# A two-block mixer, GLA and expert kernel: work of the chunked scan moved between engines, other stages reordered

## The reference

```python
def step(state, xs):                       # hgrn2_scan, per chunk
    qc, kc, vc, lfc = xs
    cum = jnp.cumsum(lfc, axis=-2)
    o_inter = einsum('bhtd,bhde->bhte', qc * exp(cum), state)
    diff = cum[:, :, :, None, :] - cum[:, :, None, :, :]
    decay = exp(where(tril[:, :, None], diff, -inf))
    scores = einsum('bhtd,bhsd,bhtsd->bhts', qc, kc, decay)
    o_intra = einsum('bhts,bhse->bhte', scores, vc)
    k_dec = kc * exp(cum_last - cum)
    state = exp(cum_last)[..., None] * state + einsum('bhsd,bhse->bhde', k_dec, vc)
```

## Time and profile before

| | us |
|---|---|
| runs before: median (lowest, highest) | 1871.67 (1871.23, 1877.39) |
| profiled execution, its own time | 1871.47 |
| its span | 1869.7 |
| PE busy | 1817.9 |
| PEld busy | 1346.8 |
| POOL busy | 978.1 |
| VectorE busy | 782.6 |
| ScalarE busy | 549.4 |

### The profile page before, as it was taken

How to read it: one execution, slowest core, us unless ns; L and a number is a source line. 1 busy time by engine, 2 the same in 40 slices (tenths; PEclk the granted TensorE clock), 3 DMA queues, 4 the chain that set the end, 5 groups by cost and what they waited for, 6 DMA issues and landing times.

```text
span 1869.7 us, 22394 instructions
## 1 busy us (share of the span) xinstructions
PE 1817.9 (97%) x9105; PEld 1346.8 (72%) x9105; DVE 782.6 (42%) x1154; ACT 549.4 (29%) x1037; POOL 978.1 (52%) x547
## 2 busy tenths in 40 slices
PE   7998999999999999999999999999999999999998
PEld 6887888788888888888777888878744444433456
DVE  4375777734524301422676565433221222221234
ACT  5534557522422101211233444332230000000025
POOL 6499958467378878897565896437500000000022
PEclk9999999999999999999999999999999999999999
DMA  6231125223123222333322322114999999999991
GB/s 210 86 90 46 46 79 181 68 68 109 39 91 92 100 101 91 102 113 92 114 79 69 90 90 83 53 57 148 387 385 410 428 427 427 428 428 427 421 373 56
DMA packets 82918, 335.83 MB, mean 180 GB/s; under 512 B 6528, under 2 KB 8320, under 8 KB 67712
## 3 DMA queue, kind: packets, MB, share of 16 engines
q1 hardware_dynamic: 79296, 322.47, 46.1%
q10 hardware_dynamic: 3520, 11.93, 1.7%
HBM read 328.08 MB, written 6.29 MB: 179 GB/s over the span
## 4 chain that ended last, share of the span: by engine, by line
PE 80%; POOL 7%; DMA 5%; DVE 4%; ACT 2%; issue 1%; SPq 0%; ACTq 0%; DVEq 0%; POOLq 0%
PE bank L669 52%; PE bank L2168 13%; PE bank L2205 3%; DMA arena<-in_w_exp_up 3%; POOL arena L1007 2%; PE bank L2187 2%; DMA shared<-in_w_exp_up 2%; POOL arena L1003 2%; PE bank L690 1%; POOL shared_r L987 1%; PE bank L2322 1%; PE bank L1192 1%; PE bank L1829 1%; PE bank L1840 1%; PE bank L1206 1%
## 5 line engine op out<-in xcount | busy, mean ns | idle before, releaser
L669 PE MATMUL bank<-shared_r 128*128 128x512 f32 (+2 forms) x3036 | 699.0, 387 | 5.6 <-DVE shared_r L767 1.8
L669 PEld LDWEIGHTS bank<-shared_r 128*128 128x128 f32 x3036 | 554.2, 188 | 122.9 <-issue 9.3
L708 POOL TENSOR_TENSOR shared_r<-shared,small 128x1024 fp32r<-128x1024 f32 (+1 forms) x134 | 260.4, 1943 | 244.4 <-PE bank L669 243.8
L709 POOL TENSOR_TENSOR shared_r<-shared,shared_r 128x1024 fp32r<-128x1024 f32 (+1 forms) x134 | 327.2, 2442 | 10.5
L708 POOL TENSOR_TENSOR spare_r<-arena,small 128x1024 fp32r<-128x1024 f32 x2 | 3.8, 1892 | 468.5 <-DMA arena<-in_w_ple_gate 468.5
L2168 PE MATMUL bank<-arena 128*64 128x512 f32 x624 | 186.6, 596 | 0.8 <-ACT arena L2260 0.5
L2168 PE MATMUL bank<-shared,arena 128*64 128x512 f32 x592 | 181.4, 602 | 6.0 <-DMA shared<-in_w_exp_up 2.9
L669 PE MATMUL bank<-shared_r,arena_r 128*128 128x512 f32 x624 | 146.0, 393 | 0.0
L669 PEld LDWEIGHTS bank<-shared_r,arena_r 128*128 128x128 f32 x624 | 117.8, 190 | 24.2
L2168 PEld LDWEIGHTS bank<-shared,arena 128*64 128x64 f32 x592 | 58.6, 139 | 91.2 <-issue 91.2
L2168 PEld LDWEIGHTS bank<-arena 128*64 128x64 f32 x624 | 59.9, 138 | 56.8 <-issue 55.6
(11 more groups left out here) (483 smaller groups left out, 2600.8 us busy)
## 6 DMA issues: line engine op xcount, KB each, us to landing
shared<-in_w_in SPq DMA_DIRECT2D x80, 512.0 KB, 3.6
shared<-in_w_exp_up SPq DMA_DIRECT2D x11, 2048.0 KB, 25.5
arena<-in_w_exp_down SPq DMA_DIRECT2D x11, 2048.0 KB, 30.1
arena<-in_w_exp_gate SPq DMA_DIRECT2D x10, 2048.0 KB, 31.2
shared<-in_w_exp_gate SPq DMA_DIRECT2D x9, 2048.0 KB, 20.8
arena<-in_w_exp_up SPq DMA_DIRECT2D x9, 2048.0 KB, 23.7
shared<-in_w_up SPq DMA_DIRECT2D x32, 512.0 KB, 3.7
shared<-in_w_down SPq DMA_DIRECT2D x32, 512.0 KB, 3.6
```

Source lines behind the costliest of these rows:

```text
L669: ins = pe.matmul(dst, W_, x_, start=first, stop=final)
L708: link(pool.tensor_tensor(hi, raw(p), small[:, 18:19].to_broadcast([P, hi.shape[1]]), ALU.add))
L709: pool.tensor_tensor(lo, raw(p), hi.bitcast(F32), ALU.subtract).then_inc(S_("w_split"), 1)
```

## The change

Scan: the largest level of chunks u = 1 to 3 is made by `first_level` on ScalarE, sixteen exponentials of 128 x 64 with a bias per partition, in place of four subtractions on POOL and one exponential; `NREF`, the negated sums at the boundary, is one small VectorE instruction before the scan. `keys_sum` for the next chunk moves from POOL to VectorE; the bank of level 3 is emptied before it. ScalarE forms the next chunk's keys behind the evacuation; POOL splits at most one part per level. Start: 18 products before the transposes, and a wait for each input where it is first used. mLSTM: the gate products of three tiles move ahead of the masks, the others behind the four cells; the two remainders of head 3 go behind two cells. GLA: `gla_squares(act, 0)` follows the evacuation, `gla_turn(0)` comes after 8 of the 12 steps, `gla_turn(1)` after 5. `wide` also takes in `proj_g` and `proj_v`.

```diff
-    wide = [... (("proj_h", "proj_m"), ("down1", "proj_g"), ("gatt", "ygla")) ...]
+    wide = [... (("proj_h", "proj_m"), ("down1", "ygla")) ...]
...
         pe.wait_ge(S_("ident"), 1)
+        keep_busy(pe, BASE["norm_mix"] + KT - 1, 18)
...
-            for kk in range(part["kp"] if ready is not None else 0):
-                if isinstance(ready, Hidden):
-                    pe.wait_ge(S_("ht_lo"), ready.first + part["k0"] + kk + 1)
-                else:
-                    bank_done(pe, ready[part["k0"] + kk])
             for g in range(panel["groups"]):
...
                 for kk in range(part["kp"]):
                     k = part["k0"] + kk
+                    if g == 0 and isinstance(ready, Hidden):
+                        pe.wait_ge(S_("ht_lo"), ready.first + k + 1)
+                    elif g == 0 and ready is not None:
+                        bank_done(pe, ready[k])
...
+        def first_level(u):
+            g, b = u * NL, LEVELS[0]
+            bank_written(act, hg_bank["level", u - 1, NL - 3])
+            act.wait_ge(S_("h_w"), 2 * u + 1)
+            q, k = HQL[g % 3], HKL[g % 3]
+            for h in range(H):
+                fwd, bwd = hg_view(CH, 0, u)[:, h], hg_view(CH, 1, u)[:, h]
+                act.activation(q[:, h, b:C], fwd[:, b:C], ACT.Exp, bias=NREF[:, 0, h, u:u + 1])
+                act.activation(q[:, h, 0:b], bwd[:, 0:b], ACT.Exp, scale=-1.0, bias=CH[:, 1, h, u, b:b + 1])
+                act.activation(k[:, h, 0:b], HW[u % 2][0][:, h, 0:b], ACT.Exp, scale=-1.0, bias=CH[:, 0, h, u, b:b + 1])
+                ins = act.activation(k[:, h, b:C], HW[u % 2][1][:, h, b:C], ACT.Exp, bias=NREF[:, 1, h, u:u + 1])
+            ins.then_inc(S_("h_e"), 1)
...
-                act.wait_ge(S_("h_d"), g + 1)
-                act.activation(HL[g % 3], HL[g % 3], ACT.Exp).then_inc(S_("h_e"), 1)
+                if l == 0 and u:
+                    first_level(u)
+                else:
+                    act.wait_ge(S_("h_d"), g + 1 - u)
+                    act.activation(HL[g % 3], HL[g % 3], ACT.Exp).then_inc(S_("h_e"), 1)
...
-                elif l == 3 and u < ST - 1:
-                    keys_of(u + 1)
...
                 hg_evacuate(act, done, hg_seen(g))
+                if l == 3 and u < ST - 1:
+                    keys_of(u + 1)
...
-                for d in range(2):
+                for d in range(2 if l or not u else 0):
...
-                ins.then_inc(S_("h_d"), 1)
-                hg_split_lo(pool, False, lo, min(14, hg_parts(hg_seen(g - 1))) if g else 1)
+                if l or not u:
+                    ins.then_inc(S_("h_d"), 1)
+                hg_split_lo(pool, False, lo, min(14, lo[0] + 1, hg_parts(hg_seen(g - 1))) if g else 1)
...
-                if l == 4 and u < ST - 1:
-                    if u:
-                        pool.wait_ge(S_("h_kd"), 2 * u - 1)
-                    keys_sum(pool, u + 1)
+                if l == NL - 1 and u < ST - 1:
                     pool.wait_ge(S_("h_w"), 2 * u + 3)
...
                 state(d, u - 1)
+            pairs(u, 3)
...
             if u < ST - 1:
+                if u:
+                    dve.wait_ge(S_("h_kd"), 2 * u - 1)
+                dve.wait_ge(S_("h_w"), 2 * u + 2)
+                keys_sum(dve, u + 1)
                 key_both(u + 1)
             query(u, 5)
-            pairs(u, 3)
...
         dve.wait_ge(S_("cols"), 1)
+        for t in range(ST - 1):
+            if t == 2:
+                dve.wait_ge(S_("conv"), 5)
+            dve.tensor_tensor(MIX[:, t, 0:512], MIX[:, t, 0:512], GATE[:, t, 0:512], ALU.mult)
...
-        link(gla_squares(act, 0))
         gla_evacuate(act, done, gla_first + gla_each * ST)
         assert done[0] == 12
+        link(gla_squares(act, 0))
...
         gla_pe(pe, steps)
-        run_steps(steps, 13)
+        run_steps(steps, 8)
         gla_turn(pe, 0)
...
-        run_steps(steps, 8)
+        run_steps(steps, 5)
         gla_turn(pe, 1)
...
         keys_sum(dve, 0)
+        dve.tensor_scalar(NREF, CH[:, :, :, :, LEVELS[0]], -1.0, None, ALU.mult)
```

More of the change, by code:

```diff
@@ L295, in part_done @@
             eng.wait_ge(part_used, parts[p]["signal"])
-    wide = [p for a, b in (("proj_h", "proj_m"), ("down1", "proj_g"), ("gatt", "ygla")) for w in range(PB[a], PB[b]) for p in panels[w]["parts"]]
+    wide = [p for a, b in (("proj_h", "proj_m"), ("down1", "ygla")) for w in range(PB[a], PB[b]) for p in panels[w]["parts"]]
     between = [p for w in range(PB["xk"], PB["out1"]) for p in panels[w]["parts"]]
@@ L365, in build @@
     HKDT = [heads(spare[:, 2 * S + S * j:2 * S + S * j + S]) for j in range(2)]
+    NREF = head_r.rearrange("p (d h c) -> p d h c", d=2, h=H)
     HQD = [heads(bc[:, 512 * i:512 * i + 512]) for i in range(2)]
@@ L1426, in mix_dve @@
                 near(h + 1)
-            if h == H - 1:
-                for d in range(2):
-                    evac_lo(dve, BASE["turn_a"] + d, XTS[:, 1, d, :], XTS[:, 0, d, :], mix_gain(d))
             for t in range(ST):
+                if h == H - 1 and t == 2:
+                    for d in range(2):
+                        evac_lo(dve, BASE["turn_a"] + d, XTS[:, 1, d, :], XTS[:, 0, d, :], mix_gain(d))
                 n = cell_out(h, t)
@@ L1440, in mix_dve @@
                 release_own(dve, dve.scalar_tensor_tensor(o, bank[:, 256:256 + C], sm_a[:, 1:2], o, ALU.mult, ALU.add), n)
-                if h == 0:
-                    if t == ST - 1:
-                        dve.wait_ge(S_("scan_sq"), 1)
-                    ins = dve.tensor_tensor(MIX[:, t, 0:512], MIX[:, t, 0:512], GATE[:, t, 0:512], ALU.mult)
-                if h == 1:
-                    if t == 0:
-                        dve.wait_ge(S_("sd_part"), 2)
-                        link(dve.reciprocal(heads_of(head_r, 0), heads_of(head_ss, 0)))
+            if h == 0:
+                dve.wait_ge(S_("scan_sq"), 1)
+                link(dve.tensor_tensor(MIX[:, ST - 1, 0:512], MIX[:, ST - 1, 0:512], GATE[:, ST - 1, 0:512], ALU.mult))
+            if h == 1:
+                dve.wait_ge(S_("sd_part"), 2)
+                link(dve.reciprocal(heads_of(head_r, 0), heads_of(head_ss, 0)))
+                for t in range(ST):
                     ins = dve.tensor_tensor(scan_half[:, t], scan_half[:, t], heads_of(head_r, 0)[:, t].unsqueeze(2).to_broadcast([P, H, C]), ALU.mult)
-            if h == 0:
-                link(ins)
-            if h == 1:
                 ins.then_inc(S_("mix_a"), 1)
```

## The result

The changed kernel takes **1891.6 us** in the median of four runs (1889.5 to 1893.1), the kernel before 1873.6 beside it: a ratio of 1.0093 with a 95% interval of 1.0072 to 1.0115. The forecast was 1854, in a range of 1847 to 1866. So the change costs 18 us where 17.5 were to be won. The profiled execution took 1891.73 us, its span is 1890.0.

The account below looks back on a forecast made before the run. POOL's queue was taken to bound the scan, through ScalarE and VectorE, and PE itself elsewhere. Terms -11.5 - 1.9 - 1.5 - 2.3 - 0.3 = -17.5 took 1871.5 to 1854 us, range 1847 to 1866.

Parts of the forecast that it names:

- the upper end of the sums' price: Scan: the keys' two additions on VectorE cost 1.4 to 5.7 us, taken as 3.
- the second rival: Scan: VectorE and POOL collide, so it gives 6 us instead of 11.5; 1859.5 us, chance 0.21.
- Scan, -11.5: Chunked scan: PE's idle 10.7 and low clock 3.4 us go, but 2.6 us of waits; bounds -14.1 and -6.
- POOL's relief: Scan: subtractions and keys' sums, 18.1 us, leave POOL's 114.5, so that 96.4 remain.
- the fourth rival: Chunk starts in the scan: sixteen small exponentials on ScalarE take 17.6 us, 33 us late in three chunks; 1884, chance 0.05.
- they end before the query of level 5, where VectorE stands idle for 5.15 us: Scan: VectorE's idle 5.15 us covers the keys' sums, taken as 3 us; without that cover PE waits.
- Start, -1.9: Kernel start: warm-up lifts the low clock, so the first product starts near 13.9 instead of 15.79 us; bounds 0 and -2.4.
- mLSTM, -1.5: mLSTM cells: gate products leave VectorE's queue, removing waits of 1.8 us for its scaling; bounds 0 and -1.8.
- Linear attention, -2.3: Linear attention: moved squares and turn remove PE's waits of 0.57 and 1.78 us; bounds -1 and -2.7.
- Slots, -0.3: Projections after the second block's first: four slots remove a 1.33 us wait, mostly replaced by VectorE's chain; bounds +1 and -1.3.
- Clock: Scan: 3.4 us lost to low clock after the gaps of 2.44 and 3.03 us go with those gaps.
- The experts' weights: Experts: if the weight stream kept its time, 17.5 us would turn into waits for weights; 1870, chance 0.07.

Follow-up runs that it names:

- hold_all: The held kernel: the whole changed kernel with four waits added to POOL's queue and nothing else; 1863.7 us, ratio 0.9945 to the kernel before.
- best3: The held kernel with VectorE's sums for the next chunk's keys moved right behind its masking of level 0; 1856.8 us, ratio 0.9908.
- h_nokeys: The held kernel without the keys' sums of chunks 3 and 4, whose keys then use stale sums; 1858.7 us.
- p_start: Only the start's edits on the kernel before: warm-up products and a wait for each tile right ahead of its products; 1870.9 us, ratio 0.9988.
- p_slots: Only the four slots, kept from the second down product to linear attention's output product, on the kernel before; 1883.2 us, ratio 1.005.
- p_mlstm: Only the mLSTM's reordering on the kernel before; 1883.2 us, ratio 1.0051.
- p_gla: Only linear attention's reordering (earlier turns, ScalarE's squares after the evacuations) on the kernel before; 1877.2 us, ratio 1.0018.
- p_scan: Only the scan's edits (biased exponentials, keys' sums on VectorE, at most one POOL split per level) on the kernel before; 1872.6 us, ratio 0.9992.
- m_columns: Only the mLSTM's reordering on the kernel before, its four 128x512 normalisations written as sixteen 128x128 products with a factor column; 1884.4 us, ratio 1.0057.
- s_poolkeys: Only the scan's edits on the kernel before, with the keys' sums left on POOL; 1869.7 us, ratio 0.9983.

## Why the prediction was wrong

Five stages, cut at the starts of the same PE instructions in the timelines (first product, memory's transposes, the transposes of line 560, the turn of queries and keys, the span's end), in us. Each column is one execution; that of `hold_all` is 3.4 us below its median:

```
stage                       before   after   hold_all   best3
start                         15.8    14.6       13.6    13.7
projections and scan         265.9   267.3      264.6   258.4
mLSTM to line 560            612.6   619.9      611.4   611.3
to the turn                   51.3    59.2       49.1    49.1
the rest                     924.1   929.0      919.9   921.3
span                        1869.7  1890.0     1858.5  1853.8
```

**The step that failed** is the same in the three terms that turned to losses (mLSTM, linear attention, slots) and is part of the scan's: VectorE's work was priced at its free duration wherever its place, or POOL's, moved. Beside POOL's splits the same instructions took 10.05 us instead of 2.50, 10.25 instead of 3.26 and 20.0 instead of 12.2 (4.1 with POOL held). The prediction had the row for the other price, 2.86 us for an addition of 0.7 beside a split. It used it in the scan, for the upper end of the sums' price and the second rival, and nowhere else. Term by term:

- *Scan, -11.5.* Measured -1.6 alone, not to be told from nothing; in its profile the stage is 0.7 us shorter. POOL's relief, the exponentials (4.2 us forecast for sixteen, 3.9 measured, none of the 33 us of the fourth rival), and ScalarE's and VectorE's earlier evacuations came as said; VectorE's, the masks of level 3 ahead of the sums and the query, is worth 6.5 us in the held kernel. What failed is "they end before the query of level 5, where VectorE stands idle for 5.15 us". That idle time was a wait for POOL, and with POOL's relief and the sums in front it was gone. In chunk 1 POOL's pairs of subtractions took 2.1 us beside the sums instead of 1.2; in chunk 2 the keys' addition behind the sums fell beside a split and took 2.87 us (1.24 in `h_nokeys` and `best3`), the next two queries 2.35. PE was late again, by 3.26 and 3.42 in place of 2.44 and 3.03. With the sums in another place the stage gives 7.5. The second rival, "gives 6 instead of 11.5", had the right mechanism, and was still too kind. The cap on the splits had no effect that can be told.
- *Start, -1.9.* Right: -2.1 alone, -1.2 to -2.2 in the profiles of the table, and PE then waits for POOL's first split, as forecast. The first product starts between 13.6 and 14.9 us in the profiles with this edit, and between 15.8 and 17.3 in those without. One size was off: the 18 products took 6.21 us, not 4, and ended at 8.09, just ahead of the first transposes.
- *mLSTM, -1.5.* Failed at "so the masks of the next head begin no later": four instructions in a row beside POOL's splits take 10.05 us, not 2.8. Measured +7.3. With POOL held the stage gives -1.2, so the gain was sized well.
- *Linear attention, -2.3.* "The price is that the turn must be ready four steps sooner" was written and not costed. The products that must be ready began 0.6 us after a split did and took 10.25 us, not 3.26. Measured +3.1 alone.
- *Slots, -0.3.* Failed at its upper bound of +1. The free slots let POOL split through the whole rotation, which took 20.0 us instead of 12.2 and so held PE for 9.93. Measured +7.9. What the fourfold slots gave (-2.2 with POOL held) is more than forecast.
- *Clock.* The gaps that were to take 3.4 us of low clock with them were replaced by longer ones; from the first product on PE's busy time rose by 4.2 instead.

The range ended at 1866 because its poor ends were those of gains that fail, not of costs that grow. The only slower case was ScalarE's. The experts' weights took little part: PE's waits for them are 7.0 us before and 9.1 after.

## What to carry to other kernels

When an edit moves a product, sum or scaling of VectorE whose large inputs all lie in SBUF, or lets POOL start work sooner, look up what POOL runs at the new time, and price the instruction at one POOL instruction each, not at its own length. A queue with free slots is not a gain by itself: POOL that runs ahead takes its time from VectorE. Four waits in its queue, at the places where PE waits for VectorE, gave back 28 us. An idle stretch that is itself a wait for the bound being removed is no cover for new work.

## What the hardware showed that was not expected

**The stall of one addition has two sizes.** The keys' addition (0.69 us when held clear) starts 0.07 to 0.10 us after a split of POOL in every run without the hold. It then takes either 2.9 or 7.6 us: it gets in behind POOL's first instruction, or only when POOL's row of six has ended. The same code in two kernels, where all differs only before it or much later (`before`: 2.86, PE's wait 1.40; `p_start`, VectorE's timeline):

```profile
128.09 7.62 DVE L1052 TENSOR_TENSOR arena<-arena 128x512 f32<-128x512 f32 x1 [4.11 <-ACT arena L914]
```

`p_slots` had 7.62 too, with PE waiting 4.29; `p_mlstm`, `p_gla`, `p_scan`, `m_columns` and `s_poolkeys` had 2.86 to 2.89. What decides was not found. PE's wait behind it is 4.3 us in the one case and at most 1.4 in the other; how much of the scatter between executions comes from it was not measured.

**The collision works both ways, but not evenly.** POOL's splits beside the row of normalisations took up to 2.34 and 2.7 us instead of 1.89 and 2.4, while VectorE's pieces took 2.5 instead of 0.69; yet short pieces of POOL (two subtractions, 1.2 us) stretched to 2.1 beside VectorE's sums. Instructions of VectorE that read PSUM kept their time beside POOL: in six of the traces (`before`, `after`, `hold_all`, `best3`, `p_slots`, `m_columns`) none took over 0.03 us more than its like without POOL. So did the small reciprocals on SBUF (0.17 us).
